# Output rows kept in open PSUM banks through an expert loop, and a gather moved ahead of the third weight piece

## What is computed

```python
h = layer_norm(ALPHA * x + mix, ln1_g, ln1_b)
# 32 experts, each row goes to its best 4, weighed by the softmax of their scores
gate, up = split(xb @ w_gu[e] + b_gu[e])          # 1024 -> 2 x 1024
gate = min(gate, 7);  up = clip(up, -7, 7)
act = (up + 1) * gate * sigmoid(1.702 * gate)
y = act @ w_down[e] + b_down[e]                    # 1024 -> 1024
x = layer_norm(ALPHA * h + sum of gate weight * y, ln2_g, ln2_b)
```

## Time and profile before

| | |
|---|---|
| median of 3 runs | 1518.57 us (1517.45 to 1519.9) |
| the profiled execution's own time | 1518.58 us |
| its span in the profile | 1516.8 us |
| PE busy | 1472.4 us (97%) |
| DVE busy | 525.0 us (35%) |
| ACT busy | 323.9 us (21%) |
| data moved by DMA | 507.81 MB |
| pieces of the loop | 128 `wGU` and 64 `wD`, 2048 KB each |
| time from issue to landing, median | 32.7 us (`wGU`), 33.4 us (`wD`) |

### The profile page before, as it was taken

One profiled execution on the slowest core, in us unless ns is written; L12 is line 12 of the kernel. 1 busy time (PEld: TensorE's weight loads), 2 busy tenths in 40 slices (PEclk: granted clock), 3 DMA queues, 4 the chain that ended last, 5 costly groups with the idle time before them and its releaser, 6 DMA issues.

```text
span 1516.8 us, 23113 instructions
## 1 busy us (share of the span) xinstructions
PE 1472.4 (97%) x9127; PEld 738.0 (49%) x9127; DVE 525.0 (35%) x1031; ACT 323.9 (21%) x824; POOL 108.3 (7%) x95
## 2 busy tenths in 40 slices
PE   9999999999999999999999999999999999999996
PEld 7777776556777764333333333333333333333332
DVE  3652788867520136222122112212212212122123
ACT  1224214631210014211211212112112112111212
POOL 1002141010402401000000000000000000000000
PEclk9999999999999999999999999999999999999999
DMA  6346687555269676999999999999999999999995
GB/s 212 111 168 177 207 267 233 179 177 189 81 217 338 254 280 250 426 417 430 426 428 428 429 428 428 429 429 429 429 429 429 429 429 429 428 429 428 429 429 213
DMA packets 110638, 507.81 MB, mean 335 GB/s; under 512 B 12608, under 2 KB 49072, under 8 KB 85904
## 3 DMA queue, kind: packets, MB, share of 16 engines
q1 hardware_dynamic: 103900, 499.64, 82.2%
q10 hardware_dynamic: 6676, 7.29, 1.6%
HBM read 491.19 MB, written 15.72 MB: 334 GB/s over the span
## 4 chain that ended last, share of the span: by engine, by line
PE 68%; DMA 19%; DVE 2%; ACT 1%; issue 1%; DVEq 0%; SPq 0%; ACTq 0%
DMA wGU<-in_w_gu 18%; PE ps L2448 14%; PE ps L2456 12%; PE ps L1925 10%; PE ps L2439 6%; PE ps L2229 4%; PE ps L2361 3%; PE ps L1939 3%; PE ps L2395 2%; PE ps L2246 2%; PE ps L2259 2%; PE ps L2369 1%; ACT xs L1273 1%; PE ps L2382 1%; PE ps L2013 1%
## 5 line engine op out<-in xcount | busy, mean ns | idle before, releaser
L2448 PE MATMUL ps<-wGU,xe 128*64 128x512 f32 x1536 | 341.7, 594 | 11.9 <-DMA wGU<-in_w_gu 11.9
L2456 PE MATMUL ps<-wD,aT 128*64 128x512 f32 x1024 | 226.8, 595 | 0.0
L2448 PEld LDWEIGHTS ps<-wGU,xe 128*64 128x64 f32 x1536 | 107.5, 137 | 226.9 <-issue 199.5
L1925 PE MATMUL ps<-xT,ring 128*128 128x288 f32 (+1 forms) x864 | 179.8, 409 | 1.2 <-PEq L200 0.7
L1925 PEld LDWEIGHTS ps<-xT,ring 128*128 128x128 f32 (+1 forms) x864 | 125.1, 170 | 46.0 <-issue 3.5
L2456 PEld LDWEIGHTS ps<-wD,aT 128*64 128x64 f32 x1024 | 70.7, 137 | 131.8 <-issue 127.9
L1825 DVE COPY ysb<-ps 64x512 f32<-64x512 f32 x32 | 22.2, 693 | 313.1 <-PE ps L2460 313.1
L1818 DVE TENSOR_SCALAR sg<-sg 128x512 f32<-128x512 f32 x32 | 13.7, 427 | 317.2 <-ACT sg L1268 317.2
L2439 PE MATMUL ps<-wGU,xe 128*64 128x512 f32 x512 | 115.7, 593 | 5.6 <-DMA wGU<-in_w_gu 5.6
L1268 ACT ACTIVATE sg<-ps 128x512 f32<-128x512 f32 x32 | 19.1, 598 | 463.1 <-PE ps L2439 463.1
L1217 ACT ACTIVATE xe<-ps,lnT 128x64 f32<-128x64 f32 x262 | 81.2, 413 | 12.9 <-PE ps L2369 12.9
(11 more groups left out here) (490 smaller groups left out, 1467.7 us busy)
## 6 DMA issues: line engine op xcount, KB each, us to landing
wGU<-in_w_gu SPq DMA_DIRECT2D x128, 2048.0 KB, 32.7
wD<-in_w_down SPq DMA_DIRECT2D x64, 2048.0 KB, 33.4
ring<-in_w_in SPq DMA_DIRECT2D x21, 2048.0 KB, 9.2
out<-hst SPq DMA_DIRECT2D x8, 1024.0 KB, 6.1
ringS<-in_ssd_proj SPq DMA_DIRECT2D x4, 2048.0 KB, 9.8
wbuf<-prompt_A_rows ACTq DMA_DIRECT2D x16, 384.0 KB, 3.8
out<-Sb SPq DMA_DIRECT2D x2, 2048.0 KB
ring<-in_hg_proj SPq DMA_DIRECT2D x2, 2048.0 KB, 8.6
```

The source lines that it names most:

```text
L1925: last = m.matmul(ps[h, b, 0:T], ring[c % 2][:, k, n * P + h.start:n * P + h.stop], xT[:, k, :], start=(k == 0), stop=(k == KD - 1))
L2448: last = m.matmul(ps[half[h], bank, :], xe[:, f, hx, :], wgu[n][:, k, col + CW * h:col + CW * h + CW], start=(i == 0 and k == 0), stop=False)
L2456: last = m.matmul(ps[half[h], B_Y, :], aT[:, k, i - 4, :], wdn[n][:, k, CW * h:CW * h + CW], start=(i == 4 and k == 0), stop=False)
```

## The change

The five outputs of the scatter now have PSUM banks of their own for the whole loop: 0, 1, 4 and 6 (`ACC`) for the prompt rows and 7 (`B_YS`) for the samples. A matmul with `start=True` opens each bank (`opened`), DVE writes the residual into it in blocks 0 and 1 (`residual`), and every scatter accumulates onto it with `start=False`. DVE's adds are gone. The other work shares the three banks that are left: gathered rows, transposed gates and block output in bank 5, the transposed activation in the gate bank, the transposed rows in the up bank.

The gather of the next rows stands ahead of the third piece (i = 2) of every block. The activation's last two steps and its transposes are cut in two halves. The down bias stands between the halves and opens the output bank. ACT alone copies the block's output. DVE's work for the next block waits until piece i = 4 is used. The last layer norm reads the banks directly: DVE's `bn_stats` for the first tile of rows, ACT's sums and squares for the others.

The diff, cut to its core:

```diff
-        B_X, B_XT, B_G, B_U, B_Y, B_S = 0, 1, 2, 3, 4, 5
-        B_GT, B_AT = B_S, B_S + 1
+        B_G, B_U, B_X = 2, 3, 5
+        B_Y, B_GT, B_EB, B_AT, B_XT = B_X, B_X, B_X, B_G, B_U
+        ACC, B_YS = (0, 1, 4, 6), 7
...
                 def run(b, odd):

+                    act.wait_ge(m_x, b + 3)
+                    a.copy(xs[:], ps[:, B_X, :]).then_inc(m_xs, 1)
                     act.wait_ge(m_u, b + 1)
                     a.activation(sg[:], ps[:, B_G, :], ACT.Sigmoid, scale=SALPHA).then_inc(m_sg, 1)
                     act.wait_ge(m_gt, b + 1)
                     a.copy(gT[:], ps[:, B_GT, 0:T]).then_inc(m_gc, 1)
-                    act.wait_ge(m_x, b + 3)
-                    act.wait_ge(m_a, b + 1)
-                    a.copy(xs[:], ps[:, B_X, :]).then_inc(m_xs, 1)
                     act.wait_ge(m_at, b + 1)
                     a.copy(aT[:].rearrange("p f h j -> p (f h j)"), ps[:, B_AT, :]).then_inc(m_ac, 1)
...
                     act.wait_ge(m_f, b * 6 + 6)
                     half = slice(BLK, 2 * BLK) if odd else slice(0, BLK)
-                    a.copy(ysb[0][half, :], ps[0:BLK, B_Y, :]).then_inc(m_yc, 1)
+                    for h in range(2):
+                        a.copy(ysb[h][half, :], ps[BLK * h:BLK * h + BLK, B_Y, :]).then_inc(m_yc, 1)
...
+                def residual(t, c):
+
+                    cols, a_cols = slice(256 * c, 256 * c + 256), slice(256 * (c % 2), 256 * (c % 2) + 256)
+                    w, b = w5[:, 256 * c + 256:256 * c + 512], xres[:, 2, cols]
+                    y = ysb[1][:, a_cols] if t == 0 else w
+                    dstep(v.tensor_tensor(y, xres[:, t, cols], w, ALU.mult))
+                    v.tensor_tensor(ps[:, ACC[2 * t + c // 2], a_cols], y, b, ALU.add)
...
+                    if start is not None:
+                        dve.wait_ge(m_op, start + 1)
+                        for c in range(4):
+                            residual(start, c)
+                        if start == 1:
+                            v.tensor_copy(ps[:, B_YS, 0:256], yq[:])
                     dve.wait_ge(m_sg, b + 1)
...
                     dve.wait_ge(m_f, b * 6 + 4)
-                    dstep(v.tensor_scalar(up[:], ps[:, B_U, :], LIMIT + 1.0, 1.0 - LIMIT, ALU.min, ALU.max))
-                    v.tensor_tensor(up[:], sg[:], up[:], ALU.mult).then_inc(m_a, 1)
-                    dve.wait_ge(m_f, b * 6 + 6)
-                    half = slice(BLK, 2 * BLK) if odd else slice(0, BLK)
-                    v.tensor_copy(ysb[1][half, :], ps[BLK:2 * BLK, B_Y, :]).then_inc(m_yc, 1)
+                    for n in range(2):
+                        gate, linear = (x.rearrange("q (p k) -> q p k", k=4)[:, :, 2 * n:2 * n + 2] for x in (sg[:], up[:]))
+                        dstep(v.tensor_scalar(linear, ps[:, B_U, :].rearrange("q (p k) -> q p k", k=4)[:, :, 2 * n:2 * n + 2],
+                                              LIMIT + 1.0, 1.0 - LIMIT, ALU.min, ALU.max))
+                        v.tensor_tensor(linear, gate, linear, ALU.mult).then_inc(m_a, 1)
...
+                def weigh2(n):
+
+                    if n >= 2:
+                        dve.wait_ge(f_v, n + 3)
+                    t, cols = n // 2, both[n % 2]
+                    return v.scalar_tensor_tensor(yout[t][:, cols], ps[:, ACC[n], :], mu2[:, t:t + 1], lnw2[:, cols], ALU.add, ALU.mult)
...
+                for n in range(2):
+                    dve.wait_ge(f_s, n + 1)
+                    lstep(v.bn_stats(bst2[:, n, :], ps[:, ACC[n], :]))
+                lstep(v.bn_aggr(mv2[:], bst2[:]))
+                v.tensor_scalar(fvar[:, 0:1], mv2[:, 1:2], LN_EPS, None, ALU.add).then_inc(f_r, 1)
+                lstep(v.tensor_scalar(mu2[:, 0:1], mv2[:, 0:1], -1.0, None, ALU.mult))
...
+                def opened(banks, cols):
+
+                    for bank in banks:
+                        last = m.matmul(ps[:, bank, cols], bg3[:, 0:P], bg3[:, cols], start=True, stop=False)
+                    return last
...
-                def turn_a():
+                def turn_a(n):

                     src = up[:].rearrange("q (p k) -> q k p", k=4)
-                    for f in range(4):
+                    for f in (2 * n, 2 * n + 1):
                         last = m.transpose(ps[:, B_AT, f * P:(f + 1) * P], src[:, f, :], ident[:])
-                    last.then_inc(m_at, 1)
+                    if n == 1:
+                        last.then_inc(m_at, 1)
...
-                def prompt(j, bank):
+                def prompt(j, stop):

                     t = j // 2
-                    return m.matmul(ps[:, bank, :], gT[:, t * P:(t + 1) * P], ysb[j % 2][:], start=True, stop=True)
...
-                def scatter(n):
-
-                    for j in range(NSC):
-                        if j >= 3:
-                            pe.wait_ge(m_sa, n + (j - 2))
-                        (prompt(j, B_S + j % 3) if j < 4 else samples(B_S + j % 3)).then_inc(m_s, 1)
...
+                    return m.matmul(ps[:, ACC[j], :], gT[:, t * P:(t + 1) * P], ysb[j % 2][:], start=False, stop=stop)
...
-                        if i == 1 and pair is not None:
+                        if i == 1 and not odd and not head:
                             pe.wait_ge(m_gc, b)
                             pe.wait_ge(m_yc, b * 2)
-                            scatter(pair * NSC)
+                            for j in range(4):
+                                prompt(j, False)
+                            samples(False)
+                        if i == 2:
+                            if odd:
+                                pe.wait_ge(m_yc, b * 2)
+                            pe.wait_ge(m_p, b + 4)
+                            gather()
+                            if head:
+                                opened(ACC[2:4], slice(0, CW))
+                                opened((B_YS,), slice(0, 256)).then_inc(m_op, 1)
...
                         if i == 4:
-                            pe.wait_ge(m_p, b + 4)
-                            gather()
-                            if pair is not None:
-                                pe.wait_ge(m_sa, pair * NSC + NSC)
+                            pe.wait_ge(m_xs, b + 2)
                             turn_g()
-                            pe.wait_ge(m_a, b + 1)
-                            turn_a()
-                            pe.wait_ge(m_xs, b + 2)
+                            pe.wait_ge(m_a, b * 2 + 1)
+                            turn_a(0)
+                            pe.wait_ge(m_gc, b + 1)
+                            for h in range(2):
+                                m.matmul(ps[half[h], B_Y, :], esel[:], bd3[:, CW * h:CW * h + CW], start=True, stop=False)
+                            pe.wait_ge(m_a, b * 2 + 2)
+                            turn_a(1)
                             turn_x()
                             pe.wait_ge(m_ac, b + 1)
...
                         if i == 3:
-                            for bank, col in ((B_G, 0), (B_U, D)):
-                                for k in range(2):
-                                    for h in range(2):
-                                        last = m.matmul(ps[half[h], bank, :], xe[:, 2 + k, 1, :],
-                                                        wgu[n][:, k, col + CW * h:col + CW * h + CW], start=False, stop=(k == 1))
-                                last.then_inc(m_u if bank == B_G else m_f, 1)
+                            for k in range(2):
+                                for h in range(2):
+                                    last = m.matmul(ps[half[h], B_G, :], xe[:, 2 + k, 1, :], wgu[n][:, k, CW * h:CW * h + CW], start=False, stop=(k == 1))
+                            last.then_inc(m_u, 1)
+                            for k in range(2):
+                                for h in range(2):
+                                    last = m.matmul(ps[half[h], B_U, :], xe[:, 2 + k, 1, :], wgu[n][:, k, D + CW * h:D + CW * h + CW], start=False, stop=(k == 1))
+                            last.then_inc(m_f, 1)
...
-                        if i == 5:
-                            for h in range(2):
-                                last = m.matmul(ps[half[h], B_Y, :], esel[:], bd3[:, CW * h:CW * h + CW], start=False, stop=True)
+                                                    start=False, stop=(i == 5 and k == 3))
...
-                warm(2, 2)
-                run(0, 0, 0, None, head=True)
...
                 pe.wait_ge(m_gc, end + 1)
+                pe.wait_ge(m_yc, end * 2 + 1)
+                prompt(0, True).then_inc(f_s, 1)
                 pe.wait_ge(m_yc, end * 2 + 2)
-                samples(B_S).then_inc(f_s, 1)
-                prompt(0, B_S + 1).then_inc(f_s, 1)
-                prompt(1, B_S + 2).then_inc(f_s, 1)
+                prompt(1, True).then_inc(f_s, 1)
```

(32 more changed lines are left out.)

137 lines of the change are left out of this document (55 added, 82 removed).

## The result

| | before | after |
|---|---|---|
| median | 1518.01 us (1516.35 to 1519.9, 4 runs) | 1528.35 us (1526.82 to 1529.65, 4 runs) |
| ratio | | 1.0059, 95% interval 1.0037 to 1.0081 |
| profiled execution, its span | 1518.58, 1516.8 us | 1528.5, 1526.8 us |

The changed kernel is 0.59% slower by the ratio, 10.3 us by the medians. The forecast was 1525.5, the profiled execution 1528.5: 3.0 more.

The account below looks back on a forecast made before the run. Weights (DMA) bound the end of the loop before; PE would bound after the change. Block 0's 7.4 and the blocks' 23.9 against 22.1 spare put the last piece 3 9.2 later: 1518.58 + 9.2 - 2.1 = 1525.7, said 1525.5, range 1516.5 to 1536.

Parts of the forecast that it names:

- PE's spare 22.1: Over the loop before, work or wait added to PE costs nothing up to 22.1 us and everything beyond it.
- The signs named: Block 0's wait 3.9, idle before activation transposes 0.7 to 0.9, pairs of blocks 57.1, hardly a `wGU` wait, end 28.5 to 30.
- the DMA's rest: In block 0, the DMA rests 4.1 and about 0.6 once more, 4.7 in all, because pieces are used later.
- Net +0.77: Each block: gather in the open costs 1.94, section saves 0.95, down bias leaving the block's end saves 0.22.
- rival (d): In every block, the strided halves cost DVE say 0.27 each, 33 us more, 1558 us; chance 0.04.
- Predicted 7.4: Block 0: wait for the row selection 3.9, gather 1.94, three opening matmuls 0.55, slower clock 1.0; bounds 6.4 to 9.
- the 0.95: Section from piece 3 to the down matmuls gets 0.95 us shorter in each block; estimates 0.90 to 1.04.
- The term that was mis-sized: Block 0: loss from a lower clock after the wait, taken as 1.0 us, bounds 0 and 2.6.
- Rival (c): Clock falls inside the blocks, 1.3 us each: 1536 us at one block in four, 1546 at every second; chance 0.11.
- Predicted -2.1: End: section and bias save 0.95 + 0.22, DVE's spared adds and reads 0.9; bounds -1.2 and -3.6.
- 9.2 - 2.1: Last piece 3 starts 9.2 us later by PE's time; the end is 2.1 us shorter.
- Rival (a): The DMA still bounds, so only its rest in block 0 is left: 1521.2 us, or 1519.5; chance 0.21.

Follow-up runs that it names:

- experiments 3 and 4: Kernel before, with three or six unread bfloat16 matmuls added ahead of piece 5 in every block: 1528.0 us with three, 1546.48 us with six.
- experiment 7: Changed kernel with the activation's last two steps and its transposes uncut, the down bias ahead of them: 1524.34 us, ratio 1.0048.
- experiment 2: Changed kernel with 17 unread bfloat16 matmuls in block 0 ahead of the gather's wait: 1524.21 us, ratio 1.0032.
- experiment 6: Changed kernel with the gather after piece 3 except in block 0, and the gates' transposes between the two down pieces: 1523.79 us, ratio 1.0024.
- the kernel in one piece: Changed kernel with the activation's last steps and transposes not cut in halves, run twice: 1524.34 us, then 1524.11 us.

## Why the prediction was right, and where its sizes were off

**The bound.** PE's spare 22.1 was right: experiments 3 and 4 give it from the kernel before, to within 0.6 in the profiles and 3.3 in the medians. The signs named came: no wait for `wGU`, 57.1 a pair to the end, the wait in block 0. Three were a little outside: the idle ahead of the first transposes is 0.63 (0.7 to 0.9 was said), the end 28.0 (28.5 to 30), and the DMA's rest stands between 610 and 616, not near 609, and is nearer 5 us long than 3 to 4.

**The block.** Net +0.77 was predicted. Measured is (57.09 - 55.57) / 2 = 0.76. The down matmuls at +6.76 lie inside +6.70 to +6.84. Half a DVE step at stride takes 0.42 as an unstrided one of its size does, and experiment 7, without halves, has the same 57.1 a pair, so rival (d) is out. 31 x 0.76 = 23.6.

**Block 0.** Predicted 7.4. Piece 3 there starts at 614.60; less the 0.95 it is 613.65, against 604.29 before: 9.4. The wait was 3.6 (3.9 predicted), gather and opening matmuls 2.7 without a fall (experiment 2: 6.62 less the 3.9 of piece 2 and the biases; 2.5 predicted), and PE came to the wait 0.3 later than I said. The term that was mis-sized is the clock: I took 1.0 with an upper bound of 2.6, and it cost 2.7. The bound came from the fall at 590, where at least 2.6 us went at 1.2 GHz. In block 0 it was 6.8 us (the clock was 0.29 and 0.05 under full in two windows of 10 us, and each us at half the clock counts half). About the first us of them fell into the wait, which ends at 605.26, and cost nothing. Against experiment 7's first profile, the gather and the opening matmuls took 2.46 longer (5.16 against 2.70) and piece 2 with the biases 0.26.

**The clock in the loop.** Rival (c) expected at least one block in four. There was one fall behind the section in 32 blocks in the first profile of after, worth 1.7, and none in the second, whose span is 1.6 shorter. So the mechanism of (c) exists, but far too rarely to decide. The rule of the Trainium skill behind that rival ("TensorE: Matmul & The Clock Gate", Part 4: PE-mode transpose) did not decide it here: with 3.3 us of transposes and waits in every block the clock stayed at 2.4 GHz in 31 of 32.

**The end.** Predicted -2.1, measured -3.3. The part before the copy was right (-1.17 against 0.95 + 0.22). What follows the copy gained 2.1 and not 0.9, and for another reason than the one I gave. Of DVE's adds before only the last, 0.71 at 1505.98, was on the chain that ended last; the earlier ones lay beside PE's scatter. What counts is when DVE can begin to normalise. Before, that was 6.41 after the copy's start (1500.64 to 1507.05), behind the scatters and adds of both tiles of rows:

```profile
1507.05 1.27 DVE L1861 SCALAR_TENSOR_TENSOR w<-w,mu,lnw 128x1024 f32<-128x1024 f32 x1
```

After, it is 3.94 (1512.77 to 1516.71), since DVE needs only the first tile's two scatters and its `bn_stats`. That is 2.47 gained, and 0.35 of it is lost again up to DVE's last step. No run here separates these parts.

**The sum.** In span: 0.95 (ahead of the change) + 9.4 + 23.6 + 1.7 - 22.1 - 3.3 = 10.25, where 10.0 was measured. Forecast were 7.1 (9.2 - 2.1). The 3.1 between the sums are +2.0 (block 0), +1.7 (the fall in the loop), +0.95 (ahead of the change), -0.3 (the blocks) and -1.2 (the end), so the misses cancelled in part.

**Rival (a), the DMA still bounds.** I took 4.7 for the DMA's rest in block 0. In experiment 7, without a fall, it is (427 - 358) x 30 / 427 = 4.8, and the five quick runs of experiment 6 lost 4.5; with the fall it is 7.9. So the price held without the fall and was too low with it. Here PE was later than either, but in experiment 6 that rest is nearly the whole loss (8.4 of 9.6 in the profile).

## What to carry to other kernels

Where a step covers another engine's chain, its own time is not what moving it gains: taking the gather away made the section only 0.95 us shorter, and its 1.94 of work then stood in the open elsewhere. Count the spare time of the engine that will be late, from its own pace and not from its share of busy time, and sum everything added against it; here 22.1 of 34.7 added us were hidden, and none of the rest. In the first block, where a chain of small steps feeds a large engine, an early consumer costs its wait, the clock after it, and the idle of the DMA, whose next pieces are issued only when old ones are used.

## What the runs showed of the hardware

- A wait of 3.6 to 3.8 us in block 0 came with 6.8 to 7.2 us at 1.2 GHz in four profiles (after twice, the kernel in one piece once, experiment 6), and with none in a fifth (the other profile of the kernel in one piece). In that fifth the clock had not fallen near 590 either; in the other four it had.
- Bfloat16 matmuls with weights of 128 columns among float32 ones with weights of 64 cost about 0.25 us for going there and back, beside 0.21 each (experiments 3 and 4).
- DVE reads and writes 256 float32 numbers in pairs with gaps of two in 0.42 to 0.43 us, as it does without gaps.
